# Two norms of a Trainium2 kernel: early chunks on unnormed activations, and TensorE in GpSimd's place for the pairs' squares

## The chip, the core and the metric

The kernel runs on one core of a Trainium2 chip. The metric is the device time of one execution in microseconds (us). Each engine (TensorE for matmuls, VectorE, ScalarE, GpSimd, and SyncE, which issues most DMAs) works its own list of instructions in order; semaphores hold one engine until another has counted up.

## The reference

The reference has two blocks over one sequence of 256 tokens with 2048 features, in fp32. The parts that matter here:

```
# block 1, after the two mixers (mLSTM and neighbourhood attention)
mixed = concat([h_a, h_b]) @ w_out
x = x + ga1 * mixed
h = rms_norm(x, g_norm2) * (1 + sc2) + sh2
u, g = split(h @ w_up)
x = x + ga2 * ((gelu(conv3(g)) * u) @ w_down)
x = rms_norm(x, g_final)
# block 2, twice: h = rms_norm(x, pre_g) * (1 + scale) + shift; y = mixer(h)
#                 x = x + gate * rms_norm(y, post_g)
# mixer 0: spatial gating unit (sgu), mixer 1: latent attention (mla), whose input projection is
cq, ckv, k_rope, z = split(h @ mla_w_in)
```

rms_norm(x, g) is x * rsqrt(mean(x * x) + eps) * g, the mean taken over the features of a token. All shifts, scales and gates (twelve vectors of 2048) come from silu(c) @ w_ada and its like.

## The kernel before

**Layout.** Activations stand transposed: 128 partitions hold features, x is 16 chunks (KC) of [128, 256 tokens]. For the matmul each normed activation is kept as two fp32r halves, high and low, beside each other (h, 16 chunks of 512 columns: T = 256 high, 256 low). Each weight piece (128 x 2048) is loaded into raw, ScalarE makes its high half (w_hi, L1141), and VectorE its low half in place of the raw one (w_lo, L1626). `split` is this step on each of the two engines; `begin(stage, j)` on both splits the piece two ahead (AHEAD = 2) and then takes the conditioning pieces that a table (ADA_SPANS, L108) puts to this slot.

**A column chunk** (L584) is one output chunk of 128 features: for each of 16 kc, high weights times [high | low] activations (512 columns, L603) and low weights times the high activations (256 columns, L604), summed in one bank of a ring of three (pm0, pm1, ps). ScalarE then copies one half of the bank (L1160) and VectorE adds the other (L1677), which frees the bank.

**Stages.** w_in and attention (ka to oa), w_out (16 chunks, each added to x by the two instructions of `residual`, L1752 and L1753), w_up0 (22 times gate and up), w_down0, w_up1, w_down1, the sgu, and in block 2's second half lat (8 chunks: the latents), mla_z (16 chunks), mla_v, the heads and mla_out. The order of each engine's list is written out by hand.

**The norm between w_out and w_up0 (norm2).** ScalarE squares the residual in pairs, VectorE adds them, TensorE adds over the partitions with a matrix of ones (`sum_squares`, L682). TensorE also folds the sums of the conditioning vectors to columns (`fold_group`, L581), then VectorE takes mean, and after ScalarE's root the reciprocal (`rsqrt_mean`, L1720 to L1722). Meanwhile TensorE runs 12 matmuls that compute nothing (`keep_running`, L705). Then `normed` on VectorE (L1734, L1742) and `modulate` on ScalarE (L1189) make the 16 chunks of h, and TensorE follows chunk by chunk with two column chunks interleaved (`column_pair`, L608).

**The norm behind the sgu (pre1).** The sgu's output is turned back by matmuls with a diagonal matrix (`post0_turn`, L947), a pair of chunks at a time; VectorE adds each pair to x (`post_pair`, L2099), ScalarE squares it (L1517), GpSimd adds the two of a pair (L1612), TensorE sums over the partitions (`pair_sum`, L953, one matmul for each pair, two for the last). Then as above, with 11 idle matmuls, and lat begins with a column pair.

**Conditioning vectors.** 384 pieces of [128, 1024] are multiplied by silu(c) and added on VectorE (L1638). After 16 of them the sum is transposed and reduced (L1642, L1643); the group for norm2 needs the first 160.

**Lines that the prediction's steps touch:** `split` L1141 and L1626, `begin` (ScalarE L1148, VectorE L1664), `first_half` L1160, `second_half` L1677, `take_group` L1652, `modulate` L1189, `rsqrt_mean` L1720; the attention waves in vb and oa start on VectorE with L1871.

## Time and profile before

| what | value |
|---|---|
| time, median of 3 runs | 2393.55 us (2391.29 to 2396.11) |
| span of the profiled execution | 2390.7 us (2390.67) |
| its own whole time | not given apart from the runs |
| instructions | 31739 |
| TensorE, VectorE, ScalarE, GpSimd busy | 98%, 78%, 47%, 0% |
| granted TensorE clock, mean | 0.991 |
| HBM read | 616.06 MB, 259 GB/s over the span |

The span goes from the first to the last instruction of one execution. A busy share counts the modelled time of matmuls, which overlap at their ends, so starts are the better measure of pace. In the timeline a row gives the start, the duration, the engine, the line, the operation and the tiles; "[0.58 <-DVE h L1742]" says that the engine sat idle for 0.58 us and what ended it. Rows with "xN" are N merged instructions.

### The profile page before, as it was taken

To read this page: it belongs to the slowest core of one execution; us is meant where nothing else is said; L and a number is where in the kernel's file an instruction comes from. 1 tells how busy PE (TensorE), PEld (TensorE's weight loads), DVE (VectorE), ACT (ScalarE), POOL (GpSimd) and SP (SyncE) were. 2 spreads that over 40 slices of the span, in tenths; PEclk is the share of its full clock that TensorE was granted. 3 is DMA by queue.
4 is the path that set the end of the run, shared out by engine and by line. 5 is a ranking of instruction groups with operands and counts; after the bars stand their busy time and mean duration, and the time that the engine had idled before them with its cause. 6 is when DMAs were issued, how large, how long until landed. Compare 5 with 4: busy or idle time off the path is not lost.

```text
span 2390.7 us, 31739 instructions
## 1 busy us (share of the span) xinstructions
PE 2354.4 (98%) x13036; PEld 2030.2 (85%) x13036; DVE 1870.1 (78%) x2046; ACT 1117.9 (47%) x1383; POOL 5.3 (0%) x11
## 2 busy tenths in 40 slices
PE   6999999999999999999999999999999999999999
PEld 3688888888888888888888888898888888889987
DVE  6889888898888678888778878778787667685754
ACT  2153445545554434555445445634555334455552
POOL 0000000000000000000000000000000000000000
PEclk8799999999999999999999999999999999999999
DMA  9999776695777688777775898766777773764343
GB/s 396 360 337 353 282 282 238 229 333 210 271 273 271 216 273 295 270 273 272 244 241 182 332 327 315 272 239 236 264 264 272 273 281 138 259 226 159 124 160 140
DMA packets 119009, 620.24 MB, mean 259 GB/s; under 512 B 13392, under 2 KB 14672, under 8 KB 76112
## 3 DMA queue, kind: packets, MB, share of 16 engines
q1 hardware_dynamic: 70560, 446.45, 52.5%
q10 hardware_dynamic: 48304, 171.76, 19.5%
q8 instruction: 103, 1.69, 0.3%
q14 instruction: 42, 0.34, 0.0%
HBM read 616.06 MB, written 2.10 MB: 259 GB/s over the span
## 4 chain that ended last, share of the span: by engine, by line
PE 92%; DVE 4%; DMA 2%; ACT 1%; issue 1%; SPq 0%; POOL 0%; DVEq 0%; POOLq 0%; ACTq 0%
PE pm L603 26%; PE ps L603 14%; PE pm L604 13%; PE ps L604 7%; PE pm L642 5%; PE pm L644 5%; PE pm L643 5%; PE ps L644 2%; PE ps L642 2%; PE ps L643 2%; DVE acc_first L1688 2%; DMA e<-in_ada 1%; DMA ada<-in_ada 1%; PE px L928 1%; DVE w_lo L1626 1%; PE px L815 1%
## 5 line engine op out<-in xcount | busy, mean ns | idle before, releaser
L1626 DVE TENSOR_TENSOR w_lo<-raw,w_hi 128x2048 fp32r<-128x2048 f32 (+2 forms) x412 | 892.3, 2166 | 354.4 <-ACT w_hi L1141 352.8
L1141 ACT ACTIVATE w_hi<-raw 128x2048 fp32r<-128x2048 f32 (+2 forms) x412 | 747.5, 1815 | 548.4 <-DMA raw<-in_w_down 119.3
L603 PE MATMUL pm<-h,w_hi 128*128 128x512 f32 x2318 | 798.8, 391 | 0.4 <-DVE ka L1677 0.2
L604 PE MATMUL pm<-h,w_lo 128*128 128x256 f32 x2318 | 640.9, 276 | 0.0
L603 PEld LDWEIGHTS pm<-h,w_hi 128*128 128x128 f32 x2318 | 435.2, 188 | 93.6 <-issue 2.2
L604 PEld LDWEIGHTS pm<-h,w_lo 128*128 128x128 f32 x2318 | 435.3, 188 | 0.2
L603 PE MATMUL ps<-h,w_hi 128*128 128x512 f32 x1186 | 410.6, 391 | 0.8 <-DVE w_lo L1626 0.8
L1638 DVE SCALAR_TENSOR_TENSOR acc<-ada,csil,acc 128x1024 f32<-128x1024 f32 x300 | 383.9, 1280 | 1.5
L604 PE MATMUL ps<-h,w_lo 128*128 128x256 f32 x1186 | 328.1, 277 | 0.0
L603 PEld LDWEIGHTS ps<-h,w_hi 128*128 128x128 f32 x1186 | 222.7, 188 | 48.8 <-issue 2.0
L604 PEld LDWEIGHTS ps<-h,w_lo 128*128 128x128 f32 x1186 | 222.7, 188 | 0.1
L603 PE MATMUL pm<-glu,w_hi 128*128 128x512 f32 x484 | 165.7, 390 | 0.0
L642 PE MATMUL pm<-w_hi,h 128*128 128x512 f32 x352 | 138.1, 392 | 0.6 <-DVE h L1742 0.6
L644 PE MATMUL pm<-w_hi,h 128*128 128x512 f32 x352 | 137.0, 389 | 0.0
L643 PE MATMUL pm<-w_lo,h 128*128 128x512 f32 x352 | 137.0, 389 | 0.0
L604 PE MATMUL pm<-glu,w_lo 128*128 128x256 f32 x484 | 133.8, 276 | 0.0
L603 PEld LDWEIGHTS pm<-glu,w_hi 128*128 128x128 f32 x484 | 90.9, 188 | 19.0
L604 PEld LDWEIGHTS pm<-glu,w_lo 128*128 128x128 f32 x484 | 90.9, 188 | 0.0
L642 PEld LDWEIGHTS pm<-w_hi,h 128*128 128x128 f32 x352 | 66.1, 188 | 15.0 <-issue 1.0
L644 PEld LDWEIGHTS pm<-w_hi,h 128*128 128x128 f32 x352 | 66.1, 188 | 13.9
L643 PEld LDWEIGHTS pm<-w_lo,h 128*128 128x128 f32 x352 | 66.1, 188 | 13.4
L603 PE MATMUL ps<-glu,w_hi 128*128 128x512 f32 x220 | 75.3, 389 | 0.0
(434 smaller groups left out, 2979.5 us busy)
## 6 DMA issues: line engine op xcount, KB each, us to landing
ada<-in_ada ACTq DMA_DIRECT2D x320, 512.0 KB, 5.5
raw<-in_w_up SPq DMA_DIRECT2D x88, 1024.0 KB, 5.0
raw<-in_w_in SPq DMA_DIRECT2D x56, 1024.0 KB, 6.2
raw<-in_w_down SPq DMA_DIRECT2D x64, 704.0 KB, 5.0
raw<-in_sgu_v SPq DMA_DIRECT2D x32, 1024.0 KB, 5.0
raw<-in_sgu_u SPq DMA_DIRECT2D x32, 1024.0 KB, 5.4
raw<-in_sgu_z SPq DMA_DIRECT2D x32, 1024.0 KB, 5.0
raw<-in_sgu_out SPq DMA_DIRECT2D x32, 1024.0 KB, 4.9
```

Source lines behind the costliest of these rows:

```text
L603: pe.matmul(dst[:, :], wh[:, k, :], hl, start=(kc == 0), stop=False, skip_group_check=True)
L604: mm = pe.matmul(dst[:, 0:T], wl[:, k, :], hi, start=False, stop=last, skip_group_check=True)
L642: pe.matmul(dst[:, :], h_hi, wh[:, k, :], start=(kc == 0), stop=False, skip_group_check=True)
L643: pe.matmul(dst[:, :], h_hi, wl[:, k, :], start=False, stop=False, skip_group_check=True)
L644: mm = pe.matmul(dst[:, :], h_lo, wh[:, k, :], start=False, stop=(kc == 4 * parts - 1), skip_group_check=True)
L815: mm = pe.matmul(px[1 + d][:, tc * DH_A:(tc + 1) * DH_A], probs, va[:, sc, hd_ * DH_A:(hd_ + 1) * DH_A], start=first, stop=last)
L928: mm = pe.matmul(px[g % 4][:, c * T + n * P:c * T + (n + 1) * P], v_sgu[:, n, g * 2 * P + c * P:g * 2 * P + (c + 1) * P], mixw[s][:, r, 0: ...
L1141: act.activation(hi_(q, n), raw_(q, n), ACT.Copy).then_inc(hi_ready, 1)
L1626: tt_(lo_(q, n), raw_(q, n), whole(hi_(q, n)), ALU.subtract).then_inc(lo_ready, 1)
L1638: ins = stt(dst, w, c, dst, ALU.mult, ALU.add)
L1688: ins = stt(dst, first_buf(p), c, dst, ALU.mult, ALU.add)
```

## The change

For norm2 and pre1 TensorE begins the next projection on activations that aren't normed yet. With gain = (1 + scale) * g, the output is rstd * (W (gain * x)) + W shift, since rstd is one number for each token. So a tile `rough` holds, for each chunk, the low half of gain * x (256 columns), its high half (256), and two more columns with the shift's high and low half. An early column chunk (`early_tile`) runs three matmuls for each kc, of 258, 256 and 258 columns. When the root is there, VectorE multiplies the bank by rstd and adds the two shift columns into a bias (`early_scale`), and ScalarE adds this bias (`early_shift`).

- w_up0: the first 6 chunks are early. ROUGH_AT makes the rough chunks behind w_out's columns 11 to 15; the fold of the group moves behind column 9; the sums of squares come nine steps into the first early chunk; the real norm chunks (h) are made in parts (UP_PARTS) behind the splits and scales of chunks 0 to 4. Chunk 6 on use h.
- lat: all 8 chunks are early. Chunks 0 and 1 run interleaved with the turns and the pairs' sums; two norm chunks are made behind each lat chunk; mla_z uses h.
- Both `keep_running` of these norms and their column pairs go, with the wait of TensorE for x after the last pair.
- GpSimd's part is gone; TensorE sums both squares of each pair.
- The conditioning pieces move: vb 24 (17), w_out 12 in 9 slots (19 in 13), w_up0 from slot 6, the last 16 from mla_z (lat).
- Tiles gpad, conv and uu move to make room.

```diff
-ADA_SPANS = [("ka", 4, 12, 18), ("va", 0, 8, 14), ("qb", 0, 16, 28), ("vb", 0, 14, 17), ("w_out", 0, 13, 19),
-             ("w_up0", 0, 40, 32), ("w_down0", 0, 32, 18), ("w_up1", 0, 44, 36), ("w_down1", 0, 26, 10), ("sgu_v", 3, 29, 40),
-             ("sgu_u", 0, 32, 24), ("sgu_z", 0, 32, 24), ("sgu_out", 0, 28, 24), ("lat", 0, 20, 16)]
+ADA_SPANS = [("ka", 4, 12, 18), ("va", 0, 8, 14), ("qb", 0, 16, 28), ("vb", 0, 15, 24), ("w_out", 0, 9, 12),
+             ("w_up0", 6, 37, 32), ("w_down0", 0, 32, 18), ("w_up1", 0, 44, 36), ("w_down1", 0, 26, 10), ("sgu_v", 3, 29, 40),
+             ("sgu_u", 0, 32, 24), ("sgu_z", 0, 32, 24), ("sgu_out", 0, 28, 24), ("mla_z", 0, 16, 16)]
-NORM_STEPS = {"norm2": 12, "pre0": 12, "pre1": 11}
-GAP_SPLITS = {"norm2": ("w_up0", 2), "pre0": ("sgu_v", 2), "pre1": ("lat", 2)}
-SPLIT_SOONER = [("w_up0", 0), ("lat", 0), ("sgu_v", 0), ("sgu_v", 1)]
+ROUGH = ["norm2", "pre1"]
+EARLY = {"w_up0": 6, "lat": 8}
+RW = 2 * T + LINE
+ROUGH_AT = {11: range(0, 3), 12: range(3, 6), 13: range(6, 9), 14: range(9, 12), 15: range(12, 15)}
+UP_PARTS = {0: range(0, 3), 1: range(3, 6), 2: range(6, 9), 3: range(9, 12), 4: range(12, 16)}
+NORM_STEPS = {"pre0": 12}
+GAP_SPLITS = {"pre0": ("sgu_v", 2), "pre1": ("lat", 2)}
+SPLIT_SOONER = [("lat", 0), ("sgu_v", 0), ("sgu_v", 1)]
...
# TensorE
+            def early_tile(stage, c, kc):
...
+                pe.matmul(dst[:, 0:T + 2], wh[:, kc, :], r[:, kc, T:2 * T + 2], start=(kc == 0), stop=False, skip_group_check=True)
+                pe.matmul(dst[:, 0:T], wh[:, kc, :], r[:, kc, 0:T], start=False, stop=False, skip_group_check=True)
+                mm = pe.matmul(dst[:, 0:T + 2], wl[:, kc, :], r[:, kc, T:2 * T + 2], start=False, stop=(kc == KC - 1), skip_group_check=True)
...
-            fold_group(1)
-            sum_squares([("norm2", 0)])
-            keep_running(NORM_STEPS["norm2"])
+                if c == 9:
+                    fold_group(1)
...
+                    for c in range(EARLY[up]):
+                        for kc in range(KC):
+                            if c == 0:
+                                rough_needed(up, kc)
+                            if (c, kc) == (0, 9):
+                                sum_squares([("norm2", 0)])
+                            early_tile(up, c, kc)
+                    for c in range(EARLY[up], COLUMNS[up][0]):
+                        columns(up, c, both(h), (lambda g: h_needed("norm2")(4 * g + 3)) if c == EARLY[up] else None)
...
             def pair_sum(p):
                 buf = pre_bufs[p % 4]
-                if p < PAIRS - 1:
-                    pe.wait_ge(pre_added, p + 1)
-                    pe.matmul(pn[:, 0:T], ones[:, :], buf[:, 0, :], start=(p == 0), stop=False).then_inc(pre_summed, 1)
...
+                pe.wait_ge(pre_sq, p + 1)
+                for j in range(2):
+                    mm = pe.matmul(pn[:, 0:T], ones[:, :], buf[:, j, :], start=(p + j == 0), stop=(p + j == PAIRS))
...
+            for p in range(3):
+                turned_pair(p)
+            for p in range(PAIRS):
+                if p + 3 < PAIRS:
+                    turned_pair(p + 3)
+                for kc in (2 * p, 2 * p + 1):
+                    rough_needed("lat", kc)
+                    for c in range(2):
+                        early_tile("lat", c, kc)
+                if p:
+                    pair_sum(p - 1)
             pair_sum(PAIRS - 1)
-            pe.wait_ge(x_ready, PAIRS)
-            keep_running(NORM_STEPS["pre1"])
-            stage_columns("lat", h_needed("pre1"))
+            for c in range(2, EARLY["lat"]):
+                for kc in range(KC):
+                    early_tile("lat", c, kc)
# ScalarE
+            def early_shift(stage, c, dst):
+                summed(stage, c)
+                act.activation(dst, dst, ACT.Identity, bias=early_bias[:, c:c + 1]).then_inc(half_out, 1)
+                act.wait_ge(half_out, halved(stage, c))
...
             for c in range(8):
                 begin("lat", c, ahead=("lat", c) not in SPLIT_SOONER)
-                first_half("lat", c, lat[:, c, :])
+                early_shift("lat", c, lat[:, c, :])
+                modulate("pre1", S1, range(2 * c, 2 * c + 2))
# VectorE
+            def early_scale(stage, c, dst):
+                dve.wait_ge(piece_done, done(stage, c))
+                tt_(dst, bank(stage, c)[:, 0:T], rstd[:, :], ALU.mult)
+                dve.tensor_reduce(early_bias[:, c:c + 1], bank(stage, c)[:, T:T + 2], AX.X, ALU.add).then_inc(freed(stage, c)[0], 1)
+            def normed_part(norm, shift, chunks):
...
+                for kc in chunks:
+                    stt(nt[:, kc % 4, :], x[:, kc, :], gain[:, k, kc:kc + 1], rstd[:, :], ALU.mult, ALU.mult).then_inc(xn_ready, 1)
+                for kc in chunks:
+                    dve.wait_ge(hh_ready, k * KC + kc + 1)
+                    stt(h[:, kc, T:2 * T], nt[:, kc % 4, :], mod(shift, kc), whole(h[:, kc, 0:T]), ALU.add, ALU.subtract).then_inc(h_ready, 1)
...
                     begin(up, 2 * i, ahead=(up, 2 * i) not in SPLIT_SOONER)
                     if i > 1:
                         gated_unit(up, i - 1, k - 1)
+                    if 2 * i < EARLY.get(up, 0):
+                        if i == 0:
+                            rsqrt_mean("norm2", D)
+                        early_scale(up, 2 * i, gpad[:, k % 2, 1:1 + T])
+                        normed_part("norm2", SH2, UP_PARTS.get(2 * i, ()))
...
                     begin(up, 2 * i + 1)
                     if i:
                         glu_low(k - 1)
+                    if 2 * i < EARLY.get(up, 0):
+                        normed_part("norm2", SH2, UP_PARTS.get(2 * i + 1, ()))
...
             rsqrt_mean("pre1", D)
-            normed("pre1", S1)
             for c in range(8):
                 begin("lat", c, ahead=("lat", c) not in SPLIT_SOONER)
-                second_half("lat", c, lat[:, c, :])
+                early_scale("lat", c, lat[:, c, :])
+                normed_part("pre1", S1, range(2 * c, 2 * c + 2))
```

## Rows read from the trace of the kernel before

**Rows 1.** Page, part 1, then part 5 (busy, mean ns, idle before and its releaser).
```profile
PE 2354.4 (98%) x13036; PEld 2030.2 (85%) x13036; DVE 1870.1 (78%) x2046; ACT 1117.9 (47%) x1383; POOL 5.3 (0%) x11
...
L1626 DVE TENSOR_TENSOR w_lo<-raw,w_hi 128x2048 fp32r<-128x2048 f32 (+2 forms) x412 | 892.3, 2166 | 354.4 <-ACT w_hi L1141 352.8
```

**Rows 2.** Timeline, TensorE, end of w_out to w_up0 chunk 8; columns: start, duration, what.
```profile
548.50 0.98 PE L581 MATMUL pv<-fold,sel 128*128 128x32 f32 x8
549.31 1.11 PE L691 MATMUL px<-ssq,ones 128*128 128x256 f32 x4
...
551.50 5.34 PE L705 MATMUL px<-par,ones 128*128 128x256 f32 x24
...
557.43 0.47 PE L621 MATMUL pm<-h,w_hi 128*128 128x512 f32 x1 [0.58 <-DVE h L1742]
...
603.71 0.39 PE L603 MATMUL pm<-h,w_hi 128*128 128x512 f32 x1
...
604.05 0.39 PE L603 MATMUL pm<-h,w_hi 128*128 128x512 f32 x1
```

**Rows 3.** Timeline, VectorE and then ScalarE, after the end of w_out.
```profile
548.70 0.48 DVE L1752 SCALAR_TENSOR_TENSOR x<-pm,mods,x 128x256 f32<-128x256 f32 x1
...
549.62 0.18 DVE L1652 TENSOR_TENSOR mods<-pv,par 128x32 f32<-128x32 f32 x1
...
556.13 1.31 ACT L1189 ACTIVATE h<-nt,mods 128x256 fp32r<-128x256 f32 x3 [2.34 <-DVE nt L1734]
```

**Rows 4.** Timeline, VectorE and then ScalarE, in w_up0.
```profile
582.53 0.42 DVE L1677 TENSOR_TENSOR gpad<-gpad,pm 128x256 f32<-128x256 f32 x1
582.87 2.28 DVE L1626 TENSOR_TENSOR w_lo<-raw,w_hi 128x2048 fp32r<-128x2048 f32 x1
585.07 1.28 DVE L1638 SCALAR_TENSOR_TENSOR acc<-ada,csil,acc 128x1024 f32<-128x1024 f32 x1
...
594.82 1.92 ACT L1141 ACTIVATE w_hi<-raw 128x2048 fp32r<-128x2048 f32 x1 [3.13 <-DMA raw<-in_w_up]
```

**Rows 5.** Timeline, TensorE, pre1, lat and mla_z.
```profile
2009.82 0.60 PE L953 MATMUL px<-nt,ones 128*128 128x256 f32 x2
2010.25 1.05 PE L947 MATMUL px<-diag,y_tok 128*128 128x128 f32 x8
2011.14 0.60 PE L953 MATMUL px<-ssq,ones 128*128 128x256 f32 x2
...
2035.36 0.40 PE L603 MATMUL pm<-h,w_hi 128*128 128x512 f32 x1
...
2074.56 0.40 PE L603 MATMUL ps<-h,w_hi 128*128 128x512 f32 x1
```

**Rows 6.** Timeline, VectorE, post_pair and the mean and root of pre1.
```profile
2005.99 2.44 DVE L2099 SCALAR_TENSOR_TENSOR x<-px,gain,x 128x256 f32<-128x256 f32 x6
...
2018.46 0.41 DVE L1720 TENSOR_SCALAR rstd<-px 128x256 f32<-128x256 f32 x1
...
2021.14 1.27 DVE L1734 SCALAR_TENSOR_TENSOR nt<-x,gain,rstd 128x256 f32<-128x256 f32 x3
```

**Rows 7.** Timeline, TensorE, two steps of three matmuls in the heads.
```profile
2217.66 0.28 PE L1046 MATMUL ps<-lat_hl,w_hi 128*128 128x256 f32 x1
...
2218.02 0.28 PE L1046 MATMUL ps<-lat_hl,w_hi 128*128 128x256 f32 x1
```

**Rows 8.** Timeline, VectorE, a wave of attention in oa, and the end of a unit.
```profile
412.53 0.76 DVE L1871 SCALAR_TENSOR_TENSOR s_b<-px,bias_b 128x256 f32<-128x256 f32 x2 [1.26 <-PE px L857]
...
474.86 1.25 DVE L1642 STREAM_TRANSPOSE ada<-acc 128x1024 f32<-128x1024 f32 x1
...
477.39 0.48 DVE L1752 SCALAR_TENSOR_TENSOR x<-pm,mods,x 128x256 f32<-128x256 f32 x1
```

**Rows 9.** Timeline, TensorE; then the windows view (engines, granted clock, DMA share, GB/s).
```profile
59.27 1.87 PE L678 MATMUL pv<-ones,acc_first 128*128 128x1 f32 x8 [3.41 <-DVE acc_first L1688]
...
57.00:67.00 10.00, 7.48 (x21) 4.26 (x22) 7.73 (x7) 1.91 (x1) 0.00 (x0) 0.50 1.02 412
```

More of the change, by code:

```diff
@@ L315, in build @@
              [at_(f"pt{j}", [P, 384], o_nt + 384 * (j - 2)) for j in (2, 3)]
+        rough = {"norm2": work("rough_up", [P, KC, RW], 7168, F32R), "pre1": work("rough_lat", [P, KC, RW], 7936, F32R)}
         pm = [ctx.enter_context(nc.psum_tensor(f"pm{b}", [P, 512], F32)) for b in range(2)]
@@ L361, in build @@
         x_ready = sem("x_ready")
+        gain_set = sem("gain_set")
+        rough_hi = sem("rough_hi")
+        rough_ready = sem("rough_ready")
         dve_step = sem("dve_step")
@@ L972, in _, with turned_pair @@
             pe.wait_ge(diag_ready, 2)
-            for p in range(PAIRS):
+            def turned_pair(p):
                 if p >= 3:
@@ L1010, in _ @@
             for c in range(MH):
-                columns("mla_z", c, both(h), late={2: latent_squares, 9: rotated_key, 14: doubled_key}.get(c))
+                columns("mla_z", c, both(h), (lambda g: h_needed("pre1")(4 * g + 3)) if c == 0 else None, late={2: latent_squares, 9: rotated_key, 14: doubled_key}.get(c))
             pe.wait_ge(lat_lo_ready, 2)
@@ L1348, in _ @@
                     pair_squares("w_out", "norm2", c // 2 - 1, x_pair(c // 2 - 1))
+                if c in ROUGH_AT:
+                    if c == min(ROUGH_AT):
+                        rough_shift("norm2", 1, SH2)
+                    summed("w_out", ROUGH_AT[c][-1])
+                    for kc in ROUGH_AT[c]:
+                        rough_high("norm2", kc)
             summed("w_out", KC - 2)
             last_square("norm2", 0)
-            split(piece(*GAP_SPLITS["norm2"]))
             summed("w_out", KC - 1)
+            rough_high("norm2", KC - 1)
             last_square("norm2", 1)
-            root("norm2")
-            modulate("norm2", SH2)
             def gated_unit(up, i, k):
@@ L1514, in _ @@
                 act.wait_ge(x_ready, p + 1)
+                if p == 0:
+                    rough_shift("pre1", 5, S1)
+                for kc in (2 * p, 2 * p + 1):
+                    rough_high("pre1", kc)
                 if p >= 4:
@@ L1932, in _ @@
                 residual("w_out", c, GA1)
-            take_group(1)
-            modulation("norm2", "g2", 0, SC2)
-            split(piece(*GAP_SPLITS["norm2"]))
-            rsqrt_mean("norm2", D)
-            normed("norm2", SH2)
+                if c in ROUGH_AT:
+                    if c == min(ROUGH_AT):
+                        take_group(1)
+                        modulation("norm2", "g2", 0, SC2)
+                        rough_shift("norm2", SH2)
+                    for kc in ROUGH_AT[c]:
+                        rough_low("norm2", kc)
+            rough_low("norm2", KC - 1)
             for j in range(2):
```

100 lines of the change are left out of this document (73 added, 27 removed).

## The prediction

> **What bounds the kernel now.** I read the page first: TensorE is busy 98% of the span [rows 1], so what the change can give is time in which TensorE waits or does filler. Then TensorE's timeline around the two norms. At norm2 the last w_out matmul is followed by the fold (549.31 - 548.50 = 0.81 us), the sums of squares (551.50 - 549.31 = 2.19), filler matmuls and a short idle (557.43 - 551.50 = 5.93), and column chunks 0 and 1 of w_up0, which follow the norm chunk by chunk; chunk 8 starts at 603.71 [rows 2]. At pre1 the turns and sums of squares start near 2004, and lat chunk 2 starts at 2035.36, the second mla_z chunk at 2074.56 [rows 5]. The third thing to see is not a TensorE row: VectorE and ScalarE pass every weight piece through each other, ScalarE's half taking 1.92 and VectorE's 585.07 - 582.87 = 2.20 to its next instruction [rows 4]; over the span VectorE stood 352.8 us waiting for ScalarE's half [rows 1]. Before, the norm's 16 chunks were done while TensorE ran filler and two chunks, with no weights behind them in those queues. The question is who pays for them now.
>
> **Pace on TensorE.** An early step has three matmuls of 258, 256 and 258 columns in place of 512 and 256. Where the trace has three of 256 columns, a step takes 2218.02 - 2217.66 = 0.36 [rows 7]; the seven chunks from lat 2 on took (2074.56 - 2035.36)/7/16 = 0.35 a pair, and w_up0 chunk 8 has 604.05 - 603.71 = 0.34 [rows 2, 5]. I take 0.355, between 0.34 and 0.36: 5.7 per chunk of 16. For 224 early steps (6 and 8 chunks) this is 0 to 4.5 us, only in so far as TensorE isn't waiting anyway. The Trainium skill ("TensorE: Matmul & The Clock Gate", Back-to-back issue gap) has a fixed 2.5 ns in every warm matmul, which for the third of each step would be an estimated 0.6 us in all; the rows show more than that.
>
> **Norm2 and w_up0.** Zero is the end of w_out; the fold is only moved ahead (0.81 on either side; by the durations below its last input is there about 1 us before column 9 ends, and if it is late, TensorE waits in w_out for what is missing), so before, chunk 8 starts at 603.71 - 549.31 = 54.4.
> - Removed: 5.93 of filler and idle, and the waits for the norm inside chunks 0 and 1.
> - TensorE alone would need 6 x 5.7 + 2.2 for the sums = 36.4 to chunk 6, and two chunks of 5.7 more, 47.8, to chunk 8: 6.6 saved.
> - But the two other engines: VectorE sees the column end 0.20 late [rows 2, 3], does the residual and the last rough halves, then splits piece 2 behind ScalarE (ScalarE free at 2.0, plus 1.92, plus 2.20) to 6.1; the squares' sum is ready at 9 x 0.355 + 2.19 + 0.2 = 5.6, so it waits. Mean, root and reciprocal take 2021.14 - 2018.46 = 2.68 [rows 6]: 8.8.
> - From there each chunk is a chain through both queues. VectorE scales (582.87 - 582.53 = 0.34 [rows 4]) and adds two columns (0.18, the nearest small sum [rows 3]): 0.55 with the handover. ScalarE adds the shift: 0.51 and 0.04 for its own wait. It then makes the high halves of the n norm chunks put there (three take 1.31 [rows 3], so 0.51 for one and the next 0.40 later), and only then comes to its next weight split (1.95), on which VectorE's split (2.20) waits, on which its next scale waits. That is 5.25 + 0.40n: 6.45 for three, 6.85 for four.
> - Along the lists: split of piece 3 done at 8.8 + 6.45 = 15.3; three norm chunks, the convolution, chunk 1's scale, shift and product 4.8: 20.1; split 4 (3.7) at 23.8; split 5 (6.45) at 30.3; low half of the product, three norm chunks, tap and split 6 (6.7) at 37.0; chunk 3's bank free at 37.5. TensorE could have begun chunk 6 at 36.4 and begins at 37.6. Product, then four norm chunks and split 7 (0.9 + 6.85): 45.3. Chunk 6 ends at 43.7 (0.4 of it a wait for the last norm chunk), so TensorE waits again; chunk 7 ends at 51.1. Saved 54.4 - 51.1 = 3.3, less 0.2 for a late bank at chunk 10: **-3.1**, between -6.6 (the chain costs nothing) and 0 (0.5 more in each of six links).
>
> **Pre1 and lat.**
> - GpSimd's seven additions go, at no gain but the waits on them; TensorE takes two sums for one, 0.43 more for each of seven pairs (2010.25 - 2009.82 [rows 5]). The first early step needs post_pair (two by 0.40 from 2005.99 [rows 6]), ScalarE's high half and VectorE's low half: about 2008.6. From there TensorE has 32 early steps (11.4), four turned pairs (2011.14 - 2010.25 = 0.89 each), eight pair sums (0.88) and about 16 changes between kinds of matmul at 0.08 (557.43 has 0.47 after the fillers, 603.71 has 0.39 [rows 2]): 23.3. The other two need only 1.7 per pair. Lat chunk 2 starts at 2031.9 where it was 2035.36: 3.4 saved here.
> - The sum is ready at 2032.1, the reciprocal at 2034.8. Then the same chain, with n = 2 and a period of 6.05, above TensorE's 5.7, and starting late: piece 2 was split ahead, but piece 3's split comes behind chunk 0's scale and norm chunks: ready at 2034.8 + 6.2 = 2041.0. Chunk 2 ends at 2037.6, **idle 3.5**. Pieces 4 to 7 follow at 6.05 each, the first mla_z piece at 2071.3. Its last four steps need norm chunks 14 and 15, which stand behind chunk 7's scale: 2034.8 + 7 x 6.05 + 2.55 = 2079.7; TensorE reaches them at 2075.5, **idle 4.2**. The second mla_z chunk starts at 2079.9 + 4 x 0.35 = 2081.3, where it was 2074.56 [rows 5]: **+6.7**. Bounds: all links hidden, TensorE is there at 2031.9 + 7 x 5.7 = 2071.8, or -2.8; 0.3 more per link, +9.
>
> **Conditioning pieces.** vb takes 24 for 17, w_out 12 for 19, one more in most of those slots: 7 x 1.28 [rows 4] and the transpose and reduction of a unit, 477.39 - 474.86 = 2.53 [rows 8]. VectorE's wait for the wave's scores was 1.26 at 412.53 [rows 8], which covers one more piece, not the piece and the turn in the slot of wave 7: +0.9, between 0 and 2.9. The loads move too: ScalarE issues seven more of 512 KB in some 80 us there, in front of its copies for the waves, which is part of that upper end. In w_out the load falls, and the rough halves (3 x 0.40 a column) take the place of a piece. mla_z takes 16 pieces in 16 slots: +0.3, 0 to 1. gain_set, the moved tiles and early_bias: nothing, small operations beside TensorE.
>
> **Sum**: -3.1 + 6.7 + 0.9 + 0.3 = +4.8 us. The profiled execution has a span of 2390.67; its own whole time isn't shown apart, the runs' median is 2.9 above the span. I add to the median: 2393.55 + 4.8 = **2398.4**. No change means within 0.2% (4.8 us) of the median, about what a measurement of this kernel can tell from none; my sum lies on that bound.
>
> **Rivals.**
> 1. The queues keep up (faster). If the chain's links overlap, -6.6 - 2.8 = -9.4: 2384; with half of the chain hidden, midway to my sum, -2.3: 2391. For it: VectorE is busy 78% of the span and ScalarE 47% [rows 1], and TensorE waits little in this kernel. Against: shares don't matter, the order does, and every link above is an instruction behind another in one queue. It decides at a period of 5.5 or less in lat, where 6.05 is worked out. 0.18.
> 2. The clock falls (slower still). The fillers are gone and two idles of 3.5 and 4.2 us stand in lat. In the trace TensorE idled 3.41 before 59.27 and the row of 57 to 67 shows the granted clock at 0.50, 1.2 GHz in place of 2.4 [rows 9]; before the idle it ran only short bursts, where in lat it streams. At half clock a stretch of ten us loses up to five; taking a loss of 2 to 5 after one of them, 2400.4 to 2403.4, well over 0.2% slower. It decides if the clock falls in either idle. The Trainium skill (same page, HAM oscillation) says that such gaps between bursts bring the clock down, and by that rule the larger idle would cost it. 0.22.
> 3. The chain is right but shorter by 0.1 to 0.5 a link, and the slots in vb cost nothing: 2391 to 2396, no change. 0.25.
> 4. My forecast, 2396 to 2401: 0.35.
>
> **How the numbers follow.** Faster: rival 1, 0.18. Of the forecast's 0.35 a good half lies above 2398.3; with rival 2 that is 0.42 and I put it at 0.44 for links that I left out. Same: the rest, 0.38. The range leaves out the full rival 1 and the last of rival 2: 2388.5 to 2404.
>
> **What would show it.** Right: TensorE's waits list gains lines on w_lo of lat pieces, a single 3 to 4 us before lat chunk 3 and one on VectorE's h low halves some 12 steps into mla_z chunk 0; w_lo splits in lat are 6.0 to 6.1 apart with VectorE waiting for ScalarE; w_up0 chunks 6 and 7 each start 1 to 2 late; the reciprocal of pre1 ends near 31 us after the first turn. Wrong: lat chunks 3 to 7 run 5.6 apart; no wait on h in mla_z; chunk 6 starts less than 36 us after w_out. The pair sums should show 16 matmuls in place of 9, and a granted clock below 1.00 after 2040 would say rival 2.

## The result, and the profile after

The changed kernel takes 2413.7 us (median of 4, 2412.26 to 2416.29), the kernel before 2393.04 (median of 4, 2391.29 to 2396.11): a ratio of 1.0074, 95% interval 1.0056 to 1.0091. That is slower, by some 20 us, and lies outside the range that was forecast. The 20 is not sharp: beside the experiments the kernel before had medians of 2394.9 to 2398.8 (13 to 26 runs each), so 2 to 6 us of it is which executions these four were. The profiled execution took 2412.26 us, with a span of 2410.5 against 2390.7.

The page of the changed kernel, part 1, then one group of part 5 (columns as in [rows 1]):

```profile
PE 2361.7 (98%) x13228; PEld 2040.5 (85%) x13228; DVE 1884.3 (78%) x2094; ACT 1128.6 (47%) x1417; POOL 0.2 (0%) x4
...
L1703 DVE TENSOR_TENSOR w_lo<-raw,w_hi 128x2048 fp32r<-128x2048 f32 (+2 forms) x412 | 892.0, 2165 | 360.4 <-ACT w_hi L1191 358.9
```

Against [rows 1] hardly anything moves: 192 more matmuls, VectorE's wait for ScalarE's high half 358.9 us for 352.8. Of 20 us the page shows nothing, as TensorE is "98% busy" in both. So the trace has to be read by place.

TensorE's timeline of the changed kernel, rows after a wait in w_up0, and then in lat and mla_z:

```profile
583.01 0.36 PE L634 MATMUL pm<-rough_up,w_hi 128*128 128x258 f32 x1 [0.27 <-DVE w_lo L1703]
...
590.01 0.50 PE L620 MATMUL pm<-h,w_hi 128*128 128x512 f32 x1 [1.08 <-DVE early_bias L1826]
...
597.99 0.47 PE L620 MATMUL ps<-h,w_hi 128*128 128x512 f32 x1 [1.74 <-DVE w_lo L1703]
...
2041.88 0.47 PE L634 MATMUL pm<-rough_lat,w_hi 128*128 128x258 f32 x1
...
2051.22 0.56 PE L634 MATMUL ps<-rough_lat,w_hi 128*128 128x258 f32 x1 [3.28 <-DVE w_lo L1703]
...
2089.63 0.50 PE L620 MATMUL pm<-h,w_hi 128*128 128x512 f32 x1 [3.06 <-DVE h L1837]
```

These are the waits that the forecast named: chunks 6 and 7 of w_up0 late by 1.08 and 1.74, lat chunk 3 by 3.28 on its low weights (3.5 forecast), mla_z chunk 0 by 3.06 on the low activations (4.2 forecast). Lat chunk 2 starts at 2041.88, 27.3 us after the last piece of sgu_out, where it was 32.2 before [rows 5]: 4.9 saved, 3.4 forecast. VectorE's timeline shows the chain behind them:

```profile
2048.78 2.29 DVE L1703 TENSOR_TENSOR w_lo<-raw,w_hi 128x2048 fp32r<-128x2048 f32 x1 [1.32 <-ACT w_hi L1191]
2050.99 0.42 DVE L1825 TENSOR_TENSOR lat<-pm,rstd 128x256 f32<-128x256 f32 x1
2051.33 0.15 DVE L1826 TENSOR_REDUCE early_bias<-pm 128x1 f32<-128x2 f32 x1
2051.39 0.87 DVE L1834 SCALAR_TENSOR_TENSOR nt<-x,gain,rstd 128x256 f32<-128x256 f32 x2
2052.59 0.88 DVE L1837 SCALAR_TENSOR_TENSOR h<-nt,mods,h 128x256 fp32r<-128x256 f32 x2 [0.33 <-ACT h L1256]
2054.80 2.29 DVE L1703 TENSOR_TENSOR w_lo<-raw,w_hi 128x2048 fp32r<-128x2048 f32 x1 [1.32 <-ACT w_hi L1191]
...
2060.81 2.29 DVE L1703 TENSOR_TENSOR w_lo<-raw,w_hi 128x2048 fp32r<-128x2048 f32 x1 [1.32 <-ACT w_hi L1191]
```

Split to split is 2054.80 - 2048.78 = 6.02 us (6.05 forecast), and in each turn VectorE stands 0.33 and 1.32 us for ScalarE. TensorE's windows view (window, length, busy and instructions, granted clock, DMA share, GB/s) has the other thing that was foreseen:

```profile
2040.00:2047.00 7.00, 7.00 (x55) 1.00 0.78 301
2050.00:2057.00 7.00, 5.78 (x27) 0.51 0.35 133
2058.00:2070.00 12.00, 12.00 (x103) 1.00 0.50 176
2091.00:2095.00 4.00, 4.00 (x16) 0.57 0.63 221
```

After each of the two waits TensorE runs at half clock, 1.2 GHz, for some microseconds. By the Trainium skill ("TensorE: Matmul & The Clock Gate", HAM oscillation) waits between bursts of matmuls do that. The trace agrees, at waits of 3.28 and 3.06 us behind streaming, though not for every wait: in e11 below one of 3.0 us at the second place was followed by a clock of 1.00.

One sign went against the forecast. Lat chunks 4 to 7 run 5.68 us apart with no wait of TensorE, where the queues take 6.02 a piece: at half clock chunk 3 took 8.6 us from its wait to the next chunk, and that put TensorE behind the splits (2.7 us at chunk 4, 1.4 at mla_z chunk 0). The 6.02 of the queues comes through only at the wait for h.

None of this makes 20 us. The rest is in places that the change doesn't touch. All engines' windows in w_down0 (840 to 900), w_up1 (1000 to 1060) and sgu_out (1860 to 1920), first of the kernel before:

```profile
840.00:900.00 60.00, 60.00 (x355) 53.06 (x354) 43.86 (x42) 22.13 (x16) 0.00 (x0) 1.00 0.81 272
1000.00:1060.00 60.00, 60.00 (x355) 53.25 (x354) 51.31 (x56) 30.98 (x41) 0.00 (x0) 1.00 0.77 273
1860.00:1920.00 60.00, 60.00 (x266) 49.71 (x265) 40.67 (x27) 23.62 (x19) 0.00 (x0) 1.00 0.75 273
```

and of the changed kernel:

```profile
840.00:900.00 60.00, 60.00 (x348) 52.73 (x347) 41.87 (x39) 22.12 (x16) 0.00 (x0) 1.00 0.79 262
1000.00:1060.00 60.00, 60.00 (x355) 53.08 (x354) 51.78 (x56) 30.21 (x38) 0.00 (x0) 1.00 0.76 273
1860.00:1920.00 60.00, 60.00 (x259) 48.35 (x258) 39.18 (x24) 20.54 (x15) 0.00 (x0) 1.00 0.74 268
```

TensorE is never idle, at full clock, and gets through 348 matmuls where it did 355, and 259 for 266. In w_up1 it is as quick as before. w_up1 reads h; w_down0 reads glu and sgu_out reads y, and these two lie in the region behind early_bias. sgu_out is another kind of stage: y is loaded as the weights of the array and w_hi and w_lo stream by, three matmuls of 512 columns a step. TensorE's timeline, two matmuls 12 apart, of the kernel before and then of the changed one:

```profile
1899.66 0.39 PE L642 MATMUL ps<-w_hi,y 128*128 128x512 f32 x1
...
1902.38 0.39 PE L642 MATMUL pm<-w_hi,y 128*128 128x512 f32 x1
```

```profile
1899.65 0.39 PE L678 MATMUL pm<-w_hi,y 128*128 128x512 f32 x1
...
1902.45 0.39 PE L678 MATMUL ps<-w_hi,y 128*128 128x512 f32 x1
```

That is 2.72 us and then 2.80, or 227 and 233 ns a matmul.

A finer measure is when a weight piece is finished. SyncE's load of the piece four on waits for that, so the starts of the loads give it for all 412 pieces. By them a w_down0 piece of 11 pairs takes 3.81 us after the change and 3.74 before (346.7 and 340 ns a pair); a piece of 16 pairs in w_up1 takes 5.44 in both (340 ns). The stages by this measure, in us, after less before: start to the end of ka -2.3; qb and kb +1.6; vb and oa +3.1; w_out and w_up0 -2.4 together (+1.5 and -3.9; 0.8 is the fold that moved from one to the other); w_down0 +2.2; w_up1 +0.9; w_down1 +2.3; sgu_v to sgu_z +1.1; **sgu_out +5.1**; lat and mla_z +7.1; mla_v, heads and mla_out +1.2. Sum 19.8. The -2.3 at the start is nothing that the change did: e4, whose code there is that of before, has it too.

### The profile page after: what moved, and what is told of

Same layout as the page of the kernel before. It is cut to its first block, busy times and chain, and to the rows that moved or that the text cites. A ratio compares the mean times of both kernels' runs of the same rounds, so it can differ in the third digit from the quotient of the medians.

```text
span 2410.5 us, 32209 instructions
## 1 busy us (share of the span) xinstructions
PE 2361.7 (98%) x13228; PEld 2040.5 (85%) x13228; DVE 1884.3 (78%) x2094; ACT 1128.6 (47%) x1417; POOL 0.2 (0%) x4
## 4 chain that ended last, share of the span: by engine, by line
PE 88%; DVE 6%; ACT 3%; DMA 2%; issue 1%; ACTq 0%; SPq 0%; DVEq 0%
PE pm L620 25%; PE ps L620 13%; PE pm L621 13%; PE ps L621 6%; PE pm L678 5%; PE pm L680 5%; PE pm L679 5%; DVE w_lo L1703 2%; PE ps L678 2%; PE ps L679 2%; PE ps L680 2%; ACT w_hi L1191 1%; DVE acc_first L1765 1%; DMA e<-in_ada 1%; DMA ada<-in_ada 1%
## 5 line engine op out<-in xcount | busy, mean ns | idle before, releaser
L1703 DVE TENSOR_TENSOR w_lo<-raw,w_hi 128x2048 fp32r<-128x2048 f32 (+2 forms) x412 | 892.0, 2165 | 360.4 <-ACT w_hi L1191 358.9
L620 PE MATMUL pm<-h,w_hi 128*128 128x512 f32 x2206 | 762.4, 392 | 6.7 <-DVE h L1837 3.1
L621 PE MATMUL pm<-h,w_lo 128*128 128x256 f32 x2206 | 610.5, 277 | 0.0
L620 PEld LDWEIGHTS pm<-h,w_hi 128*128 128x128 f32 x2206 | 414.2, 188 | 97.0 <-issue 4.8
L621 PEld LDWEIGHTS pm<-h,w_lo 128*128 128x128 f32 x2206 | 414.2, 188 | 0.2
L620 PE MATMUL ps<-h,w_hi 128*128 128x512 f32 x1138 | 395.8, 393 | 1.8 <-DVE w_lo L1703 1.7
L621 PE MATMUL ps<-h,w_lo 128*128 128x256 f32 x1138 | 315.6, 277 | 0.0
L620 PEld LDWEIGHTS ps<-h,w_hi 128*128 128x128 f32 x1138 | 214.4, 188 | 48.2 <-issue 3.0
L621 PEld LDWEIGHTS ps<-h,w_lo 128*128 128x128 f32 x1138 | 214.5, 188 | 0.1
```

What stands on the lines that cost most here:

```text
L620: pe.matmul(dst[:, :], wh[:, k, :], hl, start=(kc == 0), stop=False, skip_group_check=True)
L621: mm = pe.matmul(dst[:, 0:T], wl[:, k, :], hi, start=False, stop=last, skip_group_check=True)
L1703: tt_(lo_(q, n), raw_(q, n), whole(hi_(q, n)), ALU.subtract).then_inc(lo_ready, 1)
```

## Theory and rivals

**A, the tiles moved by 64 bytes.** early_bias takes one line of 16 elements ahead of ssq, so ssq, sqt, nt and the whole work region lie 64 bytes further than before. TensorE reads glu, y, ka and the rest from there. **B**: the slower stages come from other things that the change does there (conditioning pieces, the missing GpSimd). **E**: the loss at lat is the order of the two queues; **F**: it is the amount of work or the loads. Two more came up on the way: **C**, one placing of the operands has two paces and a stall picks one, and **D**, one placing has one pace.

## Experiments: the 64 bytes

**e1_before_pad64.** The kernel before, and nothing else:

```
         rstd = sb("rstd", [P, T])
+        unused = sb("unused", [P, 16])
```

> The kernel before with nothing but an unused tile of 16 elements (64 bytes) per partition behind rstd, where the change puts early_bias, so that the squares, nt and the whole work region lie 64 bytes further. Theory A (the 64 bytes cost TensorE time in every stage whose activations lie there): the pairs of w_down0, w_down1 and sgu_out come 6 to 7 ns later each, from 340 to about 346 ns, and the time rises by 8 to 14 us. Rival B (the slower stages come from what the change does elsewhere, such as the moved conditioning pieces or the missing GpSimd): the time stays within 2 us of before.

2412.17 us (median of 4, 2411.28 to 2414.73), against 2398.75 (median of 13, 2389.83 to 2401.68): ratio 1.0064, interval 1.0041 to 1.0087. An unused tile alone brings the kernel within 2 us of the changed one, 13.4 us above the kernel before that was measured beside it. Windows of the same three stretches:

```profile
840.00:900.00 60.00, 60.00 (x348) 52.73 (x348) 43.30 (x41) 21.36 (x16) 0.00 (x0) 1.00 0.80 267
1000.00:1060.00 60.00, 60.00 (x345) 52.60 (x344) 50.31 (x55) 29.24 (x36) 0.00 (x0) 1.00 0.74 263
1860.00:1920.00 60.00, 60.00 (x258) 48.34 (x258) 39.23 (x25) 22.35 (x15) 0.00 (x0) 1.00 0.75 269
```

w_down0 and sgu_out as A says. But w_up1, whose operands did not move, is slower too here, 345 matmuls: its pieces took 5.60 us for 5.44 (two of another placing 5.55 for 5.65). That alone is 6.5 us, and A doesn't explain it; so the 13.4 us lie in the range that A gave partly by luck.

**e2_after_no_shift.** The changed kernel with early_bias in a line that was free:

```
-        early_bias = sb("early_bias", [P, 8])
+        early_bias = at_("early_bias", [P, 8], o_hi + 2 * HSTEP + PIECE + LINE)
```

> The changed kernel with early_bias in a free line behind w_hi, so that the squares, nt and the work region lie where they lay before. Theory A: 8 to 14 us are given back, 2400 to 2406 us, and the pairs of w_down0, w_down1 and sgu_out are back at 340 ns; what is left against before is the forecast's own sum of 4.8 us and a few more. Rival B: within 2 us of the changed kernel, 2412 to 2416 us.

2401.49 us (median of 10, 2394.84 to 2408.71), ratio to before 1.0022 (1.0005 to 1.0040). About 12 us come back; w_down0, w_down1 and sgu_out are at their old lengths (120.8, 119.9, 174.1 us). B falls for these stages.

**m1_offsets.** A kernel by itself: the pair of the kernel, `matmul(bank, w_hi[h:], moving[m:m+512])` and `matmul(bank, w_lo[l:], moving[m:m+256])`, in 16 placings.

> Computes nothing of the reference: 16 chunk-like groups of 32 pairs of matmuls (512 and 256 columns, 128 x 128 weights) with the activations 0, 64, 128 or 192 bytes off and the high and the low weights 0 or 64 bytes off, three times over: alone, then beside ScalarE and VectorE at work on other tiles, then beside these and loads of 1 MB too. Theory A in its plainest form (the place of the operands in SBUF sets the pace by itself): the groups differ by 6 ns or more a pair already in the first pass, by the offset modulo 128 bytes. Rival: the first pass shows one pace for all, and the offset matters only beside the traffic of the second or third pass. If no pass tells offsets apart, neither holds and the offset works through something else.

The first pass already differs, and the next two repeat it within 0.6 ns, whatever VectorE, ScalarE and the loads do (the very first group, at the start, excepted). Some of the 16, in ns a pair by the starts of the matmuls, with m, h, l in bytes:

```
m=64  h=0  l=64: 340.4     m=0   h=0  l=64: 346.8     m=64  h=64 l=0 : 346.7
m=0   h=64 l=0 : 350.1     m=128 h=0  l=0 : 351.2     m=192 h=64 l=64: 351.2
m=64  h=0  l=0 : 353.2     m=128 h=64 l=64: 353.3     m=128 h=64 l=0 : 346.9
```

So the place of the operands sets the pace, between 340 and 353 ns, with no other engine in it. Placings that differ by one step in all three agree: (192, 64, 64) with (128, 0, 0), and (128, 64, 64) with (64, 0, 0). What counts, as far as these agree, is where activations and high weights lie as seen from the low weights. The modulus that I had expected, 128 bytes, is wrong: (0, 64, 0) and (128, 64, 0) differ.

## Experiments: one placing, two paces

**m2_states.** The same kernel, with the placing of the kernel before; groups of 32 pairs, each behind a VectorE operation of another length that TensorE waits for; then groups without a stall; then a map of places.

> Computes nothing of the reference: groups of 32 pairs (512 and 256 columns). First 32 groups with the operands placed to one another as in the kernel before (high weights 192 bytes, activations 0 bytes from the low weights' place, modulo 256), each behind a stall of another length, 64 to 560 elements of VectorE work. Then 16 groups without a stall, entered from groups with the activations 64 bytes off or the high weights 192 bytes back. Then an 8 by 8 map of places in steps of 64 bytes, each behind the same stall. Theory C (a place has two paces, 340 and 350 ns a pair, and what came before picks one, which then holds): among the 32 stalls both paces appear, and none in between for long. Rival D (one place, one pace): all 32 groups and the plain entries at 340 ns within 1 ns, and what differs between executions comes from other engines. The map tells whether the three places of the kernel before (340), of the changed kernel (346.7) and of the pieces with shifted high weights (355) come out of the places alone.

Of the 32 stalls 20 lead into 340.0 ns and 12 into 350.0, none between, and each holds to the end of its group. The length of the stall doesn't order them. TensorE's timeline, the first matmuls of two pairs 20 apart in the fourth group, then in the fifth:

```profile
53.78 0.39 PE L100 MATMUL b<-moving,w_hi 128*128 128x512 f32 x1
...
60.58 0.39 PE L100 MATMUL b<-moving,w_hi 128*128 128x512 f32 x1
...
65.81 0.40 PE L100 MATMUL b<-moving,w_hi 128*128 128x512 f32 x1
...
72.81 0.40 PE L100 MATMUL b<-moving,w_hi 128*128 128x512 f32 x1
```

20 pairs take 6.80 us, then 7.00, by the same instructions on the same data. That is theory C, and D falls. The groups without a stall gave the kernel's own three paces: 340.0 to 340.9 for the placing of before, 346.6 to 347.0 with the activations 64 bytes off (the changed kernel has 346.7), 353.2 with the high weights at the low ones' place (the pieces that the kernel calls CENTRED take 5.65 us for 16 pairs, 353). The map repeats every 256 bytes for most places, though not for all: some places have several paces. The steps of sgu_out, three matmuls of 512 columns with the activations as weights, are not in this map.

With this, e1's w_up1 is explained: it came into 350 ns and kept it for 44 chunks, also past the two CENTRED ones. If so, the 6.5 us of w_up1 hang on one stall in every execution, which could be why the kernel before ran from 2390 to 2402 us beside e1; e9 below tests that.

**m3_steer** and **m4_few** ask what leads TensorE back to 340.

> Computes nothing of the reference. 120 groups of 32 pairs in the places of the kernel before (high weights 192 bytes, activations 0), each behind a stall; the first 20 straight, then 20 each behind one chunk of 16 pairs at other places: (activations, high weights) at (0, 0), (64, 192), (128, 192), (0, 64) and (192, 192) bytes. If the phase after a stall picks one of two paces: of the first 20 about 12 at 340 and 8 at 350 ns. If a chunk at other places can lead all groups into one pace, some set of 20 is at 340 ns throughout; if nothing steers, each set has both.

> Computes nothing of the reference. 160 groups of 32 pairs in the places of the kernel before, each behind a stall, eight sets of 20: with 1, 2 or 4 pairs on activations 64 bytes off ahead of them, with 2 pairs 128 bytes off, with 1 or 4 matmuls of 512 columns alone 64 bytes off, and with 1 or 4 pairs 64 bytes off between the first 16 pairs and the second. If a few matmuls at another place are enough to lead TensorE into the quick pace: the sets with 4 pairs, perhaps with 1 or 2, at 340 ns throughout. If it takes a whole chunk: 6 to 11 of each 20 at 350 ns, as without.

Groups in the slow pace at the end, of 20 each:

```
straight                          6      1 pair, 64 bytes off, ahead of the group     0
chunk at (0, 0) ahead             8      2 pairs, 64 bytes off                        3
chunk at (0, 64) ahead           11      4 pairs, 64 bytes off                        4
chunk at (64, 192) ahead          0      2 pairs, 128 bytes off                       4
chunk at (128, 192) ahead         0      1 / 4 wide matmuls alone, 64 bytes off   1 / 5
chunk at (192, 192) ahead         0      1 / 4 pairs between the two chunks       0 / 0
```

My guess, that more steering matmuls steer better, was wrong. Directly behind the stall two or four pairs only shift the odds, and why one pair there left none slow stays open. Between two chunks, with TensorE already in a pace, one pair is enough: of the 20 groups 6 had come into the slow pace, and all 6 left it; with four pairs 5 of 5 did. No quick group became slow. One group of m4, TensorE's timeline:

```profile
1583.59 0.50 PE L115 MATMUL b<-moving,w_hi 128*128 128x512 f32 x1 [0.53 <-DVE d_out L136]
...
1585.45 0.40 PE L115 MATMUL b<-moving,w_hi 128*128 128x512 f32 x1
...
1588.95 0.40 PE L115 MATMUL b<-moving,w_hi 128*128 128x512 f32 x1
...
1589.30 0.39 PE L101 MATMUL b<-moving,w_hi 128*128 128x512 f32 x1
...
1589.64 0.39 PE L115 MATMUL b<-moving,w_hi 128*128 128x512 f32 x1
...
1593.05 0.39 PE L115 MATMUL b<-moving,w_hi 128*128 128x512 f32 x1
```

Ten pairs take 3.50 us, then comes the one pair at the other place (L101), and then ten take 3.41. It costs 0.34 us.

## Experiments: the parts of the change

Nothing is moved in these; early_bias stands in the free line.

**e3_up_only** keeps the hunks of w_out and w_up0 and the three spans of pieces; **e4_lat_only** keeps those of pre1, lat and the last span; **e5_pieces_only** is the kernel before with

```
-("vb", 0, 14, 17), ("w_out", 0, 13, 19), ("w_up0", 0, 40, 32)
+("vb", 0, 15, 24), ("w_out", 0, 9, 12),  ("w_up0", 6, 37, 32)
```

> The kernel before with the part at the up projection alone (six early chunks, the norm behind them, the conditioning spans of vb, w_out and w_up0 as in the change, early_bias in a free line so that nothing moves); the latent projection and GpSimd's adding of squares stay as before. If the parts add up: w_out and w_up0 together 3 to 4 us shorter than before, vb and oa together 1 to 2 us longer, lat and mla_z as before within 0.5 us; the time between 2 us below and 1 us above before. Rival (the up part carries the loss by the conditioning pieces it crowds into vb and oa): above before by 3 us or more.

> The kernel before with the part at the latent projection alone (early chunks, TensorE adding the squares in pairs, the norm behind them, the last conditioning pieces under mla_z), nothing moved. If the parts add up: lat and mla_z together 6 to 8 us longer than before, all stages up to w_up1 within 0.5 us of before; the time 5 to 8 us above before. Rival (the loss at lat needs the up part too, or came from moved tiles): within 2 us of before.

> The kernel before with nothing changed but the slots of the conditioning pieces of vb, w_out and w_up0 (24, 12 and 32 pieces from slots 0, 0 and 6 instead of 17, 19 and 32). If the denser pieces alone make VectorE late in vb and oa: vb and oa together 1 to 2.5 us longer than before. If it takes the rest of the change: within 0.3 us of before there.

Stages in us by the ends of their pieces:

```
              before   e3_up   e4_lat   e5_pieces   e2_both, unmoved
vb + oa       110.42   112.40  110.42   112.57      112.42
w_out         89.30    90.19   89.28    89.27       90.20
w_up0         251.05   247.13  251.06   250.21      247.11
w_up1         239.79   246.47  239.79   246.36      240.33
lat + mla_z   159.30   159.30  167.69   158.54      165.85
```

w_up1 is the pace again: 246.4 where it fell into 350 ns. Apart from it the parts add up. The up part gives 3.92 and takes 0.89 in w_out, net -3.0, and +2.0 in oa. The lat part costs 6.6 (e2) to 8.4 (e4); of the difference 1.3 is mla_z chunk 1, as the half clock behind the second idle lasts 6.8 us in e4 and 3.4 in e2. e5 shows that the pieces alone make the 2 us in vb and oa. TensorE's waits in the stretch 360 to 560 of e5 (what waited for what: us, times, longest) have one line that before has not:

```profile
PE px L835 <- DVE s_b L1860: 1.6, 1, 1.6
```

Times: e3 2397.09 us (10 runs, 2391.50 to 2403.77), ratio 0.9994 (0.9980 to 1.0008), e4 2402.08 (10, 2398.21 to 2410.11), ratio 1.0022 (1.0006 to 1.0038), e5 2400.21 (one run). Beside a median before of 2397.58 (19 runs) these are -0.5 and +4.5 us. For e4 the stages say more than expected and the median less: with a pace left to chance, medians of ten are good to a few us only, and I go by the stages.

**e6_lat_order**, on top of e2. ScalarE's loop over lat, then VectorE's:

```
+                if c < 7: split(piece("lat", 0) + c + 3)          # was c + 2
                 early_shift("lat", c, lat[:, c, :])
                 modulate("pre1", S1, LAT_PARTS[c])                 # 2 2 2 2 3 3 2 0 chunks
...
                 early_scale("lat", c, lat[:, c, :])
+                if c == 0: split(piece("lat", 3))
+                normed_products("pre1", LAT_PARTS[c])
+                if 0 < c < 7: split(piece("lat", 0) + c + 3)
+                normed_lows("pre1", S1, LAT_PARTS[c])
```

> The changed kernel with nothing moved, and in lat another order: ScalarE splits three pieces ahead instead of two, VectorE makes the two or three products first, then the low weights, then the low activations, so that it no longer waits for ScalarE's high weights in each chunk; lat 3 is split before the norm's products; the last chunks are normed by lat 6. Theory E (the 6.6 to 8.4 us at lat are a chain of 6.02 us a chunk from ScalarE to VectorE and back, started late by the norm): the idle time before lat 3 falls from over 3 us to under 1, mla_z chunk 0 from 11.1 us to under 6.5, lat and mla_z together 8 to 11 us shorter than with the old order. Rival F (the loads of the weights or the amount of work, not its order, set that pace): under 3 us of it come back.

VectorE's timeline, two turns of the loop:

```profile
2045.95 2.28 DVE L1706 TENSOR_TENSOR w_lo<-raw,w_hi 128x2048 fp32r<-128x2048 f32 x1
2048.15 0.87 DVE L1849 SCALAR_TENSOR_TENSOR h<-nt,mods,h 128x256 fp32r<-128x256 f32 x2
2048.94 0.41 DVE L1828 TENSOR_TENSOR lat<-ps,rstd 128x256 f32<-128x256 f32 x1
2049.28 0.15 DVE L1829 TENSOR_REDUCE early_bias<-ps 128x1 f32<-128x2 f32 x1
2049.34 0.87 DVE L1837 SCALAR_TENSOR_TENSOR nt<-x,gain,rstd 128x256 f32<-128x256 f32 x2
2050.13 2.28 DVE L1706 TENSOR_TENSOR w_lo<-raw,w_hi 128x2048 fp32r<-128x2048 f32 x1
```

The same work, in 4.18 us a turn, with no wait for ScalarE. lat chunk 3 takes 5.81 us (10.79 in e2), mla_z chunk 0 5.47 (11.14); lat and mla_z together 155.43 us: 10.4 less than e2, 3.9 less than before. Theory E holds: the order cost 10 us, not the work. About 1.6 of them are the half clock behind the second idle, which goes with the idle: the granted clock is 1.00 throughout lat and mla_z here. 2395.43 us (10 runs, 2389.92 to 2405.40), ratio 0.9998 (0.9981 to 1.0014).

**e7_spread**, on top of e6: `("vb", 0, 15, 21), ("w_out", 0, 9, 15)`.

> As the kernel before in this call, and of the 24 conditioning pieces of vb and oa three go to w_out (21 and 15). If the 2.0 us in oa come from the pieces packed there: oa at most 1 us longer than before instead of 2. If from something else: no change in oa. w_out may lose up to 0.5 us.

vb and oa fall from 112.56 to 110.56 us, and w_out rises from 90.20 to 91.37, since TensorE now waits 0.9 us there for the fold: more than expected, 0.8 gained in all. 2393.29 us (10 runs, 2387.40 to 2399.10).

**e8_rough_576**, on top of e6: `work("rough_lat", [P, KC, 2 * T + 4 * LINE], ...)`.

> As the first of this call, with the unnormed activations of lat 576 instead of 528 elements apart, so that every chunk of them lies at the same place modulo 256 bytes (the constants of the heads are loaded a stage later to make room). If the places explain why the early triples take 355 ns: lat 3 to 7 at 340 to 350 ns a triple (5.44 to 5.60 us a chunk instead of 5.68), 0.5 to 2 us less in lat. If not: 5.68 us again.

A miss: 5.76 us a chunk where it was 5.68. The step of three matmuls has places of its own, which I didn't map. The time can't tell: 2392.04 us (10 runs, 2388.88 to 2404.65).

## Experiments: the pace no longer left to chance

Four kernels with this ahead of the first pair of a few chunks (the target is written over by the chunk's own first matmul):

```
+                    if (stage, c) in STEER:
+                        hs = h.rearrange("p a b -> p (a b)")
+                        pe.matmul(dst[:, :], wh[:, 0, :], hs[:, LINE:2 * T + LINE], start=True, stop=False, ...)
+                        pe.matmul(dst[:, 0:T], wl[:, 0, :], hs[:, LINE:T + LINE], start=True, stop=False, ...)
```

**e9_before_steered** is the kernel before, **e10_pad64_steered** e1, **e11_after_steered** the changed kernel, **e12_best_steered** e7.

> The kernel before with seven extra pairs of matmuls on activations 64 bytes off, each ahead of one chunk behind a stall (w_up0 3 and 5, w_up1 1, sgu_u 3, sgu_z 1, lat 2, mla_z 5), written over at once: 7 x 0.34 = 2.4 us of more work. Theory C (a stall picks the pace, a pair elsewhere resets it): every w_up1 at 5.44 us a chunk, lat and the end of mla_z too, and the executions, 2390 to 2402 without, within some 5 us of each other near 2392. If the spread has another cause: it stays, and all are 2.4 us later.

> The same with the unused 64 bytes in front of the squares (the kernel before, moved and steered). Theory A: w_down0, w_down1 and sgu_out stay slower (346.7 ns a pair), for their activations moved; w_up1, sgu_u and lat at 5.44 us a chunk. 10 to 12 us over the steered kernel in place, 2401 to 2404.

> The changed kernel, steered at six chunks (w_up0 9, w_up1 1, sgu_u 3, sgu_z 1, mla_z 1 and 5). As its profile had w_up1 in the quick pace already, little is to be had: 2408 to 2414 us, the executions closer to each other.

> The changed kernel with nothing moved, the order in lat mended, three conditioning pieces taken out of oa, and steered at the same six chunks. If the parts add up as their ledgers say (up part 3.0 given, 1 to 2 lost in oa and w_out, lat and mla_z 4 below before, pace no longer at random, 2 us of extra pairs): 2385 to 2390 us, 3 to 6 us under the steered kernel before.

| kernel | median us (runs) | lowest to highest | ratio to the plain kernel before, interval |
|---|---|---|---|
| before, plain | 2398.22 (26) | 2389.84 to 2409.15 | |
| e9 before, steered | 2393.84 (12) | 2390.96 to 2396.72 | 0.9980 (0.9968 to 0.9993) |
| e10 64 bytes off, steered | 2405.00 (12) | 2403.09 to 2406.64 | 1.0027 (1.0012 to 1.0042) |
| e11 changed, steered | 2411.41 (6) | 2410.64 to 2412.71 | 1.0054 (1.0034 to 1.0073) |
| e12 mended, steered | 2388.70 (9) | 2386.23 to 2390.75 | 0.9960 (0.9945 to 0.9974) |

The spread of the kernel before, 19 us over 26 runs, shrinks to 6 with seven extra pairs, and the median falls although there is more work. e10 lies 1 us above its range, e11 and e12 in theirs. e10's profile caught a case: the first chunk of w_up1 at 5.60 us, the second, steered and with 0.34 us of extra pair in it, at 5.79, then 5.44 throughout (5.65 for the CENTRED ones). e12's shows the same. The windows of e10:

```profile
840.00:900.00 60.00, 60.00 (x347) 52.72 (x347) 43.16 (x41) 21.92 (x16) 0.00 (x0) 1.00 0.81 267
1000.00:1060.00 60.00, 60.00 (x355) 53.06 (x354) 51.48 (x56) 30.59 (x38) 0.00 (x0) 1.00 0.77 272
1860.00:1920.00 60.00, 60.00 (x259) 48.35 (x258) 38.98 (x24) 21.24 (x15) 0.00 (x0) 1.00 0.75 270
```

The middle row is back at 355 (345 in e1), the other two are not, for their activations are still moved. Now the sums can be read off: 64 bytes cost 2405.00 - 2393.84 = 11.2 us, the change's own parts 2411.41 - 2405.00 = 6.4 (with six extra pairs for seven, so 0.3 too low).

## Why the prediction was wrong

**The step that failed** is in the paragraph on the conditioning pieces: "gain_set, the moved tiles and early_bias: nothing, small operations beside TensorE". I costed the instruction that writes early_bias and not the 64 bytes that it takes. Those moved the operands of eight stages: by e10 less e9, +0.7 in qb, +0.9 in kb, +0.8 in w_out, +2.2 in w_down0, +1.6 in w_down1, +5.1 in sgu_out, +0.6 in mla_v, and -0.9 in the heads, where the new place is the better one. That is 11.0 us, and 11.2 by the medians, nearly all in stages whose code the diff leaves alone. (The two profiled executions differ by 9.7 in all, since e10's reached the end of qa 2.4 earlier; that part differs by as much between executions of kernels with the same code there.) It stood in the sum as zero, and no rival had it. For 3.8 of it, in w_down0 and w_down1, m2 has the pace of that placing by itself; the 5.1 of sgu_out rest on e1 and e10 alone, where nothing but the place differs. The two paces of one placing stood in the prediction's own rows, 0.35 a pair behind lat 2 and 0.34 in w_up0, and it took them for the range of one cost.

The other terms, against the changed kernel:
- **Norm2 and w_up0, -3.1**: w_out and w_up0 -3.0 in e3 and e2. The waits were 0.27, 1.08 and 1.74, where I had about 1.2 before chunk 6 and 1.6 before chunk 7. Chunk 6 starts 37.4 us after w_out (37.6 forecast). Right.
- **Pre1 and lat, +6.7** (and mla_z's pieces, +0.3): +6.6 in e2, +7.1 in the changed kernel, +8.4 in e4. The chain was named with its period (6.02 for 6.05) and its two idles (3.28 for 3.5, 3.06 for 4.2, 4.0 in e2). The mechanism is right, and e6 shows that it is the order, as the text had it; the size is partly luck. Lat chunk 2 started 1.5 us earlier than forecast (4.9 saved for 3.4), and the half clock behind the second idle, which the sum left to a rival, took about as much (1.6 in e2, 1.7 in the changed kernel). And lat chunks 4 to 7 did not wait for their splits, as told above.
- **Conditioning pieces, +0.9 within 0 to 2.9**: 2.2 in e5, 2.0 in e2 and e3, 2.4 in e11 less e10. The mechanism was right, VectorE late for a wave behind the turn of a unit; the size was too small by half, with one wait of 1.6 us in each of these. A second, of 0.63 us in vb, is in the changed kernel alone.
- **Sum +4.8**: the parts by themselves measured 6.4 (e11 less e10), 5.9 between the profiled spans of e2 and before. Of the miss of 2413.7 - 2398.4 = 15.3 us, 11.2 are the place, 6.4 - 4.8 = 1.6 are this, 2.3 more went when the changed kernel was steered, and 0.3 is the base (2393.84 for 2393.55).
- **Rival 2, the clock**: its mechanism came true, 0.51 and 0.57 granted behind the two idles, at less than its price of 2 to 5 us. The first took some 2.9 us in lat chunk 3, but only shortened the waits behind it, since the queues set when h was ready. The second is worth 1.7 us, 1.4 of it in mla_z chunk 1 (6.98 us for 5.60); in e11 it did not come.
- **Rival 1, the queues keep up**, was false of this order and true of e6's, where the period is 4.18.
- **The bound of 0.2%** was narrower than the spread of one kernel: 19 us is 0.8%.

Not settled: why a placing has two paces and what at a stall picks one; why 0.8 to 1.4 us more lie behind the last store of the output in the six kernels with the up part that aren't steered (after, e2, e3, e6, e7, e8), and not in e11 and e12; and what places would suit steps of three matmuls, the early ones and those of sgu_out.

## What to carry to other kernels

When a change allocates anything in front of existing tiles, look at what moves behind it, and put new small tiles at the end or in a gap; where TensorE streams without idling, count its instructions in equal windows of stages that the change doesn't touch. Where an engine hands work to another and back within one loop, order each queue so that it first does what the other waits for and last what it waits for itself: here that was 10 us for no work less. And before a difference under 1% is believed, look whether the kernel has more than one pace by itself; with one pair of matmuls at a shifted address behind the stalls, the mended kernel was 0.4% faster than the kernel before (0.2%, 5.1 us, than the kernel before steered likewise) and its runs lay within 5 us.

## What was not expected of the hardware

- The pace of back-to-back fp32r pairs (512 and 256 columns) depends on the relative place of the three operands in SBUF in steps of 64 bytes: 340.4 to 353.3 ns in m1, at a granted clock of 1.00 and with no other engine at work. The Trainium skill ("TensorE: Matmul & The Clock Gate", Back-to-back issue gap) gives, for a warm matmul by itself, N / 2.4 GHz and a fixed 2.5 ns; that would make an estimated 325 ns for a pair, and no run here was under 340.
- One placing has two stable paces, 340.0 and 350.0 ns. A stall of any length tried picks between them (12 of 32 slow), and without another stall or matmuls at another place none was seen to end. Not every other place ends it: e1's w_up1 stayed slow for 44 chunks, two of them with the high weights 64 bytes on.
- A single pair with the activations 64 bytes off, amid a stream, led all 6 slow groups of 20 back to 340.0 ns (four pairs, 5 of 5); 2 or 4 pairs directly behind the stall left 3 and 4 of 20 slow.
